# The second of three chunks of each FFN down projection as two 26-product bodies, its moving sums made during the first chunk

## What is computed

```
D_MODEL = 1024; D_FF = 2816          # 8 and 22 tiles of 128
def conv_ffn(x, w_in, conv_w, conv_b, w_out):
    h = causal_dwconv(x @ w_in, conv_w, conv_b)
    gate, val = h[..., :D_FF], h[..., D_FF:]
    return (jax.nn.gelu(gate) * val) @ w_out
# first two FFNs:  h = layer_norm(DN_ALPHA * h + ffn, ...)
# last two FFNs:   x = x + _rmsnorm(f, ...)
```

## Time and profile before

| what | us |
|---|---|
| median of 3 runs (lowest, highest) | 3247.04 (3244.92, 3248.99) |
| profiled execution | 3243.14 |
| its span | 3241.4 |
| PE busy / DVE / ACT / POOL | 3174.3 / 1897.4 / 1075.4 / 1547.0 |
| granted TensorE clock, mean | 0.996 |
| chain of work through L2671 (rank bodies) | 28% |
| chain of work through L2717 (quad bodies) | 27% |

### The profile page before, as it was taken

How to read it: one execution, slowest core, us unless ns; L and a number is a source line. 1 busy time by engine, 2 the same in 40 slices (tenths; PEclk the granted TensorE clock), 3 DMA queues, 4 the chain that set the end, 5 groups by cost and what they waited for, 6 DMA issues and landing times.

```text
span 3241.4 us, 49907 instructions
## 1 busy us (share of the span) xinstructions
PE 3174.3 (98%) x16674; PEld 2552.6 (79%) x16674; DVE 1897.4 (59%) x3860; ACT 1075.4 (33%) x2383; POOL 1547.0 (48%) x1383
## 2 busy tenths in 40 slices
PE   8999999999999999999999999999999999999998
PEld 7787888867777888886446888878888688788887
DVE  6686767455555576746447555466763534376754
ACT  3533333133333233313326343123331334223322
POOL 4343887423221388642001434448863432478843
PEclk9999999999999999999999999999999999999999
DMA  3223222211111222221210111223232211222231
GB/s 133 85 85 124 79 90 99 81 57 59 59 53 40 98 85 98 103 80 47 72 46 27 65 58 59 79 78 105 85 104 72 68 57 66 79 79 85 98 104 53
DMA packets 68767, 250.60 MB, mean 77 GB/s; under 512 B 7568, under 2 KB 7568, under 8 KB 68544
## 3 DMA queue, kind: packets, MB, share of 16 engines
q1 hardware_dynamic: 68544, 247.72, 22.2%
HBM read 245.59 MB, written 2.10 MB: 76 GB/s over the span
## 4 chain that ended last, share of the span: by engine, by line
PE 91%; DVE 4%; ACT 2%; issue 2%; DMA 0%; DVEq 0%; POOL 0%; SPq 0%; ACTq 0%; POOLq 0%
PE psum L2671 28%; PE psum L2717 27%; PE psum L780 6%; PE psum L2608 5%; PE psum L2902 4%; PE psum L2199 3%; PE psum L1732 3%; PE psum L1759 2%; PE psum L812 1%; PE psum L2224 1%; PE psum L2914 1%; PE psum L1786 1%; PE psum L850 1%; DVE stream L3344 1%; ACT scratch L1446 1%
## 5 line engine op out<-in xcount | busy, mean ns | idle before, releaser
L3778 POOL TENSOR_TENSOR scratch<-scratch 128x512 f32<-128x512 f32 (+1 forms) x440 | 471.1, 1081 | 126.7 <-DVE scratch L3463 57.8
L2671 PE MATMUL psum<-scratch 128*128 128x256 f32 (+2 forms) x2080 | 506.4, 382 | 0.1
L2671 PEld LDWEIGHTS psum<-scratch 128*128 128x128 f32 x2080 | 394.3, 190 | 60.6 <-DVE scratch L3512 2.4
L3512 DVE TENSOR_TENSOR scratch<-scratch,psum 128x256 f32<-128x256 f32 (+2 forms) x720 | 299.1, 422 | 201.6 <-PE psum L2671 181.7
L2717 PE MATMUL psum<-scratch 128*128 128x256 f32 (+2 forms) x1856 | 414.3, 381 | 0.2
L2717 PEld LDWEIGHTS psum<-scratch 128*128 128x128 f32 x1856 | 352.5, 190 | 52.0 <-issue 1.6
L3480 DVE SCALAR_TENSOR_TENSOR psum<-scratch,params,psum 128x256 f32<-128x256 f32 (+2 forms) x704 | 312.8, 486 | 55.8 <-ACT psum L3088 55.8
L2990 ACT ACTIVATE scratch<-psum 128x256 f32<-128x256 f32 (+2 forms) x216 | 82.5, 385 | 553.0 <-PE psum L2717 523.0
L3715 POOL TENSOR_TENSOR scratch<-w_ring 128x512 f32<-128x512 f32 (+2 forms) x56 | 69.8, 1246 | 410.4 <-PE psum L2717 183.0
L3108 ACT ACTIVATE scratch<-psum 128x256 f32<-128x256 f32 (+2 forms) x320 | 122.8, 385 | 382.6 <-PE psum L2671 378.5
L2717 PE MATMUL psum<-acts,scratch 128*128 128x256 f32 (+2 forms) x976 | 223.1, 384 | 5.7 <-DVE stream L3344 4.5
(11 more groups left out here) (541 smaller groups left out, 6029.6 us busy)
## 6 DMA issues: line engine op xcount, KB each, us to landing
w_ring<-units SPq DMA_DIRECT2D x335, 512.0 KB, 3.6
scratch<-units SPq DMA_DIRECT2D x128, 512.0 KB, 4.3
residual<-x_t SPq DMA_DIRECT2D x4, 528.0 KB, 6.7
out_t<-residual SPq DMA_DIRECT2D x2, 512.0 KB, 3.4
out_t<-residual SPq DMA_DIRECT2D x1, 768.0 KB, 4.4
params<-cols SPq DMA_DIRECT2D x1, 568.5 KB, 10.9
out_t<-residual SPq DMA_DIRECT2D x1, 256.0 KB, 3.3
gate_w_sb<-gate_w SPq DMA_DIRECT2D x1, 96.0 KB, 10.6
```

The source lines that it names most:

```text
L2671: mm = nc.tensor.matmul(PS[:, bank, 0:H], weights(q), moving(q), start=(opens and q == 0), stop=(q == 1), skip_group_check=True)
L3512: v.tensor_tensor(row, row, PS[:, rank_bank(j, at), 0:H], ALU.add if sign > 0 else ALU.subtract).then_inc(r_later, 1)
L3778: g.tensor_tensor(blocks([RANK_BUFFERS + o for o, _, _ in sums]), blocks([a for _, a, _ in sums]), blocks([e for _, _, e in sums]), ALU.ad ...
```

## The change

The second chunk of each down projection (part 1, counted from 0) is computed by two rank bodies, 11 and 12 of the FFN, over A's tiles 8 to 15, in place of two quad bodies.

- PE runs `rank` twice in place of `quads`. The first waits for the banks as the quads of the first chunk leave them; the third chunk's quads wait for the last terms of the ranks.
- DVE's `along` is now called in both bodies of the first chunk, and makes the 20 moving sums of the second chunk: 0 to 7 between the convolutions, 8 and 9 ahead of "22" in the first body, 10 to 13 ahead of "11", 14 to 17 ahead of "21" and 18 and 19 ahead of "22" in the second. Some lie in other places than those of the up projection (`rank_v`).
- All 26 terms of a body are added to Z or subtracted from it by DVE in `rank_down`, straight out of PSUM. ScalarE takes no part. The third chunk's four moving sums stand behind the terms of products 5, 11, 17 and 23 of the first body (DOWN_AT).
- POOL makes 18 sums a body in place of 8. For the first of the two it starts as each ring buffer's quad sum has been used.
- On ScalarE and DVE the third chunk's two bodies are written out, where a register loop ran before.
- Counters of the semaphores, the release of weight slots and the numbering of bodies follow.

The core of the diff:

```diff
+RANK_ALL = RANK_UP + 2
...
+DOWN_AT = (5, 11, 17, 23)
+RANK_BODIES = (1, 2, 3, 4, 5, 6, 7, 8, 9, 10, 13, 14)
...
-for _name, _up, _ks in [("lru_out", 0, (8, 4)), ("ffn0", 1, (8, 8, 6)), ("fox_out", 0, (8,)), ("ffn1", 1, (8, 8, 6)),
-                        ("mix_out", 0, (8, 8)), ("ffn2", 1, (8, 8, 6)), ("gla_out", 0, (8,)), ("ffn3", 1, (8, 8, 6))]:
+for _name, _up, _ks in [("lru_out", 0, (8, 4)), ("ffn0", 1, (8, 0, 6)), ("fox_out", 0, (8,)), ("ffn1", 1, (8, 0, 6)),
+                        ("mix_out", 0, (8, 8)), ("ffn2", 1, (8, 0, 6)), ("gla_out", 0, (8,)), ("ffn3", 1, (8, 0, 6))]:
     BODIES[_name], CHUNKS[_name] = _b, len(CHUNK_LAST)
     if _up:
         _b += _up
         CHUNK_LAST.append(_b - 1)
...
         def rank_later(n, j, at):
-            return R_LATER + len(RANK_LATER) * rank_body(n, j) + sum(a <= at for a, _, _ in RANK_LATER)
-
-        def rank_moved(n, at):
-            return R_MOVING + len(RANK_MOVING) * n + at + 1
+            added = RANK_LATER if j <= RANK_UP else RANK_FIRSTS + RANK_LATER
+            return (R_LATER + len(RANK_LATER) * rank_body(n, j) + len(RANK_FIRSTS) * (2 * n + max(j - RANK_UP - 1, 0))
+                    + sum(a <= at for a, _, _ in added))
...
+            if down and place >= 8:
+                if place < 10:
+                    return (NORM_MU, NORM_R)[place - 8][:, 0:2 * H].rearrange("p (k t) -> p k t", k=2)
+                return scratch((19952, 4256, 2128, 2656, 3184, 3712, 0, 528, 1056)[place - 10], 2, H)
...
             def rank_terms_done(n, j, at):
 
-                if any(a == at for a, _, _ in RANK_FIRSTS):
+                if any(a == at for a, _, _ in RANK_FIRSTS) and j <= RANK_UP:
                     pe.wait_ge(r_first, rank_first(n, j, at))
-                if any(a == at for a, _, _ in RANK_LATER):
+                if any(a == at for a, _, _ in RANK_LATER) or RANK_TERMS[at] and j > RANK_UP:
...
                         for i in range(2):
-                            quads(i, b + 2 * c, u0 + KD * c, count // 2, T, chunk + c, moving, after=FFNS.index(name) if i + c == 0 else None)
+                            if c == 1:
+                                rank(n, RANK_UP + 1 + i, moving, T // 2)
+                                continue
+                            after = (n, RANK_ALL if c else RANK_UP) if i == 0 else None
+                            quads(i, b + (2 if c else 0), u0 + KD * c, count // 2, T, chunk + c, moving, after=after)
                         continue
...
                     if name in FFNS and c == 0:
                         body(1, b)
+                        continue
+                    if name in FFNS and c == 1:
+                        continue
+                    if name in FFNS:
+                        body(0, b + 2)
+                        body(1, b + 2)
                         continue
...
                     if name in FFNS and part == 1:
-                        dve.wait_ge(*when(name, "act", 2 * NF))
-                        for n in range(1, 5):
-                            moving(chunk + part + 1, n, KS[name][part + 1] // 2, acts_of(part + 1, name), H, T)
+                        rank_down()
+                        continue
...
                     def body(i, along=None):
-                        if part > 0:
+                        if name in FFNS and part > 0:
+                            dve.wait_ge(r_later, rank_later(FFNS.index(name), RANK_UP + 1 + i, RANK - 1))
+                        elif part > 0:
                             dve.wait_ge(q_added, add_done(i, b + 2 * (part - 1), "12", 1))
                         for what, p, n in (("11", 2, 1), ("21", 4, 4), ("22", 5, 3), ("12", 3, 2)):
                             if along:
-                                along(what)
+                                along(i, what)
...
-                def rank_moving(q):
+                def rank_moving(q, down=False):
 
                     op, first, second = RANK_MOVING[q]
-                    a, z = [src(2 * at, 2 * at + 2, half * H, half * H + H) if kind == "x" else rank_v(n, at, H) for kind, at, half in (first, second)]
+                    side, of = (T_out // 2, acts_of(1, name)) if down else (H, src)
+                    a, z = [of(2 * at, 2 * at + 2, half * side, half * side + side) if kind == "x" else rank_v(n, at, side, down)
+                            for kind, at, half in (first, second)]
                     for kind, at, half in (first, second):
                         if kind == "v":
-                            dve.wait_ge(r_moving, rank_moved(n, at))
-                    if q in V_PLACES[15:]:
+                            dve.wait_ge(r_moving, rank_moved(n, at, down))
+                    if q in V_PLACES[15:] and not down:
                         dve.wait_ge(q_added, add_done(0, b, "12", 1))
-                    into = rank_v(n, q, H)
+                    if q in V_PLACES[12:16] and down:
+                        dve.wait_ge(*when(name, "conv", 8 * RANK_UP))
+                    if q in V_PLACES[16:] and down:
+                        dve.wait_ge(*when(name, "conv", 8 * RANK_UP + 8))
+                    into = rank_v(n, q, side, down)
...
-                def along(what):
-
-                    if what == "11":
+                def along(i, what):
+
+                    if i == 0 and what == "11":
                         convolved(RANK_UP, 0)
                         dve.wait_ge(*when(name, "act", 4 * KD))
                         dve.wait_ge(r_product, rank_done(n, RANK_UP, RANK - 1))
-                        moving(chunk + 2, 1, KD // 2, acts_of(1, name), T_out // 2, T_out)
+                        rank_moving(0, True)
                         gated(RANK_UP, 0)
-                    if what == "21":
+                        rank_moving(1, True)
+                    if i == 0 and what == "21":
                         for s in range(1, 4):
                             convolved(RANK_UP, s)
-                            moving(chunk + 2, s + 1, KD // 2, acts_of(1, name), T_out // 2, T_out)
+                            rank_moving(2 * s, True)
                             gated(RANK_UP, s)
-
-                down(name, T_out, along)
+                            rank_moving(2 * s + 1, True)
+                    for q in {(0, "22"): (8, 9), (1, "11"): (10, 11, 12, 13), (1, "21"): (14, 15, 16, 17), (1, "22"): (18, 19)}.get((i, what), ()):
+                        rank_moving(q, True)
+
+                def rank_down():
+
+                    dve.sem_inc(q_moving, 4)
+                    dve.wait_ge(*when(name, "act", 2 * NF))
+                    for i in range(2):
+                        j = RANK_UP + 1 + i
+                        dve.wait_ge(q_added, add_done(i, b + 1, "12", 1))
+                        for at in range(RANK):
+                            for m, half, sign in RANK_TERMS[at]:
+                                dve.wait_ge(r_product, rank_done(n, j, at))
+                                earlier = [a for a, row, side in sorted(RANK_FIRSTS + RANK_LATER) if (row, side) == (m, half) and a < at]
+                                if earlier:
+                                    dve.wait_ge(r_later, rank_later(n, j, earlier[-1]))
+                                side = T_out // 2
+                                z = Z[:, 4 * i + m, half * side:half * side + side]
+                                v.tensor_tensor(z, z, PS[:, rank_bank(j, at), 0:side], ALU.add if sign > 0 else ALU.subtract).then_inc(r_later, 1)
+                            if i == 0 and at in DOWN_AT:
+                                moving(chunk + 3, 1 + DOWN_AT.index(at), KS[name][2] // 2, acts_of(2, name), T_out // 2, T_out)
+
+                down(name, T_out, along, rank_down)
...
 
-                b, u0 = BODIES[f"ffn{n}"], UNITS[f"ffn{n}"] + FFN_BODY * j
+                opening = j in (1, RANK_UP + 1)
+                b, u0 = BODIES[f"ffn{n}"] + (2 if j > RANK_UP else 0), UNITS[f"ffn{n}"] + FFN_BODY * RANK_BODIES[j - 1]
                 held = (W if SLOT[u0] < SLOTS else WX)[:, 0:SLOTS].rearrange("p s k n -> p (s k n)").rearrange("p (b f) -> p b f", f=2 * P)
...
+                if opening:
+                    pool.wait_ge(q_weight, weight_ready(0, b, 4, 1))
                 if j == 1:
...
-                        if j > 1 and RANK_LAST_USE[buffer]:
+                        if not opening and RANK_LAST_USE[buffer]:
                             pool.wait_ge(r_product, rank_done(n, j - 1, RANK_LAST_USE[buffer] - 1))
-                        if j == 1:
+                        if opening:
                             keep, q = [nq for nq, place in SUM_PLACE.items() if place == buffer // 2][0]
...
                     if name in FFNS:
                         for i in range(2):
-                            weights(0, b + 2 * part + i, u0 + KD * part + FFN_BODY * i, count // 2, FFNS.index(name) if i + part == 0 else None)
+                            if part == 1:
```

(4 more changed lines are left out.)

51 lines of the change are left out of this document (30 added, 21 removed).

## The result

| | us |
|---|---|
| changed kernel, median of 4 runs (lowest, highest) | 3227.64 (3225.43, 3231.51) |
| kernel before, median of 4 runs (lowest, highest) | 3245.98 (3243.66, 3248.99) |
| ratio, 95% interval | 0.9944 (0.9927 to 0.9961) |
| changed kernel, profiled execution (before) | 3228.54 (3243.14) |
| its span (before) | 3227.0 (3241.4) |

Between the two profiled executions the gain is 14.6 us; between the medians it is 18.3. Which of the two is the kernel's is the first question of the experiments.

The account below looks back on a forecast made before the run. PE, busy 98% of the span, was taken as the bound. The terms -16.4 + 1.0 + 1.2 + 1.6 - 0.4 = -13.0 us, from the median 3247.04, gave 3234.0 us; range 3229 to 3242.

Parts of the forecast that it names:

- 8 matmuls a chunk less, and the waits of the quads that go: Second chunk of each FFN: 104 matmuls replace 112 and the wait for DVE's two-step add goes; -16.4 us.
- (1): First-chunk bodies: two moving sums ahead of "22" make product 3 late in FFN 0 and 1; +1.0 us.
- (2): Start of the new ranks: PE waits for DVE, a quarter of the up projection's opening waits; +1.2 us.
- (3): First rank body: the third chunk's moving sums return banks late, PE waits 0.2 us twice per FFN; +1.6 us.
- (4): Third chunk: written out of register loops, it loses some of the sequencer step in front of "22"; -0.4 us.
- Rival (A): First-chunk ends: sums in front of "22" take the gain, 3243.8 us; chance 0.14 together with other local waits.
- Rival (B): Inside the ranks: DVE becomes the bound, with adds of 1.16 us the kernel is slower, 3295 us; chance 0.05.

Follow-up runs that it names:

- both_moved: Changed kernel with the third chunk's four moving sums behind products 14 and 20 of both rank bodies, and sums 8, 9, 18, 19 a step earlier; 3227.00 us.
- loops_alone: Kernel before, with only the second and third chunks' bodies written out on ScalarE and DVE in place of register loops; 3246.14 us, ratio 1.0007.
- late_sums: Changed kernel with moving sums 10 to 13 also in front of "22" of the first body, six there in place of two; 3258.96 us.
- two_more_adds: Changed kernel with two more DVE adds for each of the 208 rank terms, written to PSUM columns nobody reads; 3334.78 us.
- one_more_add: Changed kernel with one more DVE add for each of the 208 rank terms, written to PSUM columns nobody reads; 3253.10 us.
- late_sums_two: Changed kernel with only moving sums 10 and 11 also in front of "22" of the first body, four there in all; 3246.89 us.

## Why the forecast was right and wrong

The four FFNs' chunks, from the start of a chunk's first PE instruction to that of the next chunk's (third chunk: to the end of its last), us before and after:

| | first chunk | second chunk | third chunk |
|---|---|---|---|
| FFN 0 | 50.55, 50.97 | 50.60, 46.69 | 37.98, 37.94 |
| FFN 1 | 49.13, 49.29 | 49.25, 45.64 | 37.21, 36.88 |
| FFN 2 | 48.35, 48.35 | 49.25, 45.60 | 37.82, 37.80 |
| FFN 3 | 48.35, 48.35 | 49.25, 45.60 | 37.79, 37.80 |

The forecast's terms from these, with the second chunks of both_moved (46.28 us in FFN 0, 44.89 in the others) as what PE alone takes:

| step | forecast us | measured us |
|---|---|---|
| 8 matmuls a chunk less, and the waits of the quads that go | -16.4 | -17.4 |
| (1) first chunk, sums in front of "22" | +1.0 | +0.6 |
| (2) opening of the ranks | +1.2 | 0.0 |
| (3) banks behind the moving sums | +1.6 | +2.6 |
| (4) third chunk | -0.4 | -0.4 |
| sum | -13.0 | -14.6 |

The first row is 50.60 - 46.28 = 4.32 us in FFN 0 and 49.25 - 44.89 = 4.36 in each of the others. Row (3) is what the changed kernel's second chunks take beyond 46.28 and 44.89: 0.41, 0.75, 0.71 and 0.71.

**What failed.** The measured median lies 6.4 us below the 3234.0 that was forecast. The base was off, and four of the five terms were.
First, the terms: the kernel's gain in the traces is 14.6 us and the sum had 13.0. The opening of the ranks (2) was put at +1.2 and cost nothing; the removed chunk was worth 17.4 and not 16.4; (1) was 0.4 too dear; (3) was 1.0 too cheap. On balance that is 1.6 us, and it is luck that the errors partly cancel: the sum is nearer than its terms.
Second, the base. I made the sum against the profiled execution, 3243.14, noted that it lay 3.9 us below the median of three, and added it to the median. 16 further runs of the kernel before, on another chip, have their median at 3243.38; from it the same sum gives 3230.4, inside the range. In the comparison of the result itself the median of before is 3245.98, 1.1 below the base.
Third, the range's lower end was the least cost of every step (-17.5) and held nothing for the spread of what is measured. Single executions of either kernel spread over 5 to 7 us, the gain was 18.3 us in one comparison and 14.1 in the next, where the changed kernel's median is 3229.30, inside the range. Two or three us below -17.5 belonged in the range whatever the mechanism.
The 3.7 us by which the first comparison exceeds its own traces stand in no trace; the second comparison doesn't repeat them, and no more is known of them.

**By the steps.** The removed matmuls: right in kind, 1.0 us too small. The ranks run at the pitch of the quads (0.4317) and not at that of FFN 2's up projection (0.4328), whose stretch held some of their opening's waits; that is 0.5 us. The rest is the end of the second chunk in FFN 2 and 3, set 0.23 us too early as shown above. So the waits that went with the quads were 3.5 us and not 2.6. 
(1) The place was right: in FFN 1 the first step of "22" now starts as the second of the two sums ends, and PE waits 0.24 us there in place of 0.14 (20.96 now and 20.86 before for 12 products of 4 x 0.4317 = 20.72). The first step of "22" and the POOL sum beside it in the changed kernel (start us, us):

```profile
1371.61 0.68 DVE L3497 TENSOR_TENSOR norm_r<-acts 128x512 f32<-128x512 f32 x1
1372.21 0.41 DVE L3367 SCALAR_TENSOR_TENSOR stream<-residual,psum 128x256 f32<-128x256 f32 x1
1372.65 1.04 DVE L3368 TENSOR_TENSOR stream<-scratch,stream 128x256 f32<-128x256 f32 x1
...
1372.04 1.37 POOL L3772 TENSOR_TENSOR scratch<-w_ring 128x512 f32<-128x512 f32 x1 [12.61 <-PE psum L2728]
```

I had let POOL and the second step be pushed back by the whole delay. POOL started 0.43 us after DVE's last sum had, not at its end, and that last sum still took 0.68 us. The first step came 0.23 us later than before (19.33 in place of 19.10 us after the first quad), the second (L3368) took 1.04 us where it had been 1.16, and 0.1 was left. In FFN 0 product 3 came 0.06 us later.
That is not all of the +0.6. The first chunk of FFN 0 is 0.42 us longer, mostly at the end of its second body, where PE waits for the "22" of the other quad, which it didn't before. In both_moved, with no sum in front of "22", the first chunks of FFN 0 and 1 are 50.85 and 49.46 us, 0.3 longer than before in each. The second step of that "22" in FFN 0, before and then in the changed kernel with POOL's rank sums beside it:

```profile
601.74 0.83 DVE L3344 TENSOR_TENSOR stream<-scratch,stream 128x264 f32<-128x264 f32 x1
...
600.89 1.56 DVE L3368 TENSOR_TENSOR stream<-scratch,stream 128x264 f32<-128x264 f32 x1
...
598.68 3.47 POOL L3837 TENSOR_TENSOR scratch<-scratch 128x512 f32<-128x512 f32 x3 [5.70 <-PE psum L2728]
```

So part of what the first chunk costs comes from where POOL's first rank sums fall beside DVE's "22", and for this the forecast's sum had no term. This is read from the traces; no run has moved POOL's sums. 

(2) This step failed: it was read from the wrong analogue. In the up projection's opening DVE has other work between the terms; here it had the terms and two short moving sums, and the first 18 products ran in 15.55 us, 0.432 a matmul, without a wait. The count of POOL's sums in advance was right: no wait for POOL. 
(3) Right in kind, with the places exchanged. I took 1.82 us for a sum beside POOL and expected waits behind terms 5 and 11 and none behind 17, where "POOL has finished the body's sums". In FFN 2 the sums behind 5 and 11 took 0.95 and 1.14 us though POOL was busy; the one behind 17 took 1.94, as POOL had finished and gone on with the next body's sums 1.5 us before. PE waited once a rank chunk and not twice, and the one wait, 0.4 us in the view of waits, made the chunk 0.71 us longer than the 44.89 us of both_moved. Two slips: a sum beside POOL is no fixed double, it ended 0.81 us after the POOL instruction in flight did and took 0.95 where that left it alone; and of an engine that is said to be done it must be asked what stands next in its queue. 
(4) The number came out, the reason for it didn't, so this is luck. loops_alone gives the four third chunks less than 0.1 us together; in the changed kernel they gain 0.4, nearly all in FFN 1 (37.21 to 36.88). I have not tested what gives it.

Rival (A) fell: "22" came 0.1 us late and not 2.7. late_sums shows that it was a real danger with its price understated: the 2.6 to 6.4 us that I would have counted for four more sums were 4.7 to 5.2, and another 1.4 to 3.3 came from the clock. Rival (B) was priced rightly where DVE is well behind (two_more_adds) and stayed away for the reason given; the 208 new adds are as short as those read before:

```profile
L3613 DVE TENSOR_TENSOR stream<-stream,psum x208: 406/421/431, 605.7 to 3172.6; 128x256 f32<-128x256 f32 x78, 128x264 f32<-128x264 f32 x26
```

## What to carry to other kernels

Where one engine fills the span, count what is taken from it at its undisturbed pitch, and then look only at waits that another engine could put into it, each at its place in the queue. A DVE sum of two SBUF inputs that begins while a POOL sum is in flight can last until 0.81 us (at 768 elements) after the end of that one, 1.94 us in place of 0.95 here, so it belongs behind a step that nobody needs soon: here moving four such sums behind other terms gave back 0.7 us in three of the four FFNs and 0.4 in the other. And a range needs a part for the spread of the runs themselves, next to the bounds of the terms, above all when the base is a median of three.

## What was not expected of the hardware

A wait that is put into a busy TensorE can cost more than its length. After a wait of 4.7 us the granted clock was 0.50, then 0.57 in the mean, over 6.6 us in FFN 2, and the matmuls behind took 3.3 us more; after 2.4 us it fell once (1.9 us more) and once not (0.2 us). Waits of 0.4 to 0.5 us, as in the changed kernel, left it at 1.00, and so did those of up to 1.2 us in one_more_add. But a wait cost 0.2 to 0.3 us beyond its length even then: 0.4 us made 0.71 in the changed kernel's second chunk, and 2.4 us made 2.6 in FFN 3 of late_sums_two. In all, waits of 19.8 us cost 29.5 and waits of 11.9 us cost 18.8. The Trainium skill (TensorE: Matmul & The Clock Gate, "HAM oscillation — how this bites in real kernels") describes such a fall after a wait for data, and these rows agree; that 2.4 us can be enough is theirs to say.
